# Layer 0's attention with the Hyena tiles in three parts per unit pair, and the filter's taps, norm and spectrum issued behind the first K tile

## The chip, the cores and the metric

The program runs on one core of one Trainium2 chip. The metric is the device time in microseconds (us) of one execution. TensorE (PE; PEld is its weight load), VectorE (DVE), ScalarE (ACT), GpSimd (POOL) and SyncE (SP) run programs of their own, written by hand, and meet only in semaphores.

## The reference, cut to what matters

Two blocks over 256 tokens of width 1024: two layers of a three-branch block (layer 0 also carries 256 context tokens, so 512 columns), then a second block. What the change touches is the beginning of layer 0:

```python
sh, sc, gt = modulation(c, ada_w[l], ada_b[l])          # silu(cond) @ ada_w: tiles "ada"
h  = rms_norm(x, norm_pre[l]) * (1.0 + sc[:, None]) + sh[:, None]
z  = h @ w_in[l]                                        # tiles k, q, v, hy, gu, gv, gate
y_a = diff_head_out(diff_attend(q, k_all, v_all, lam), da_subln[l], lam_init)
# hyena_filter: three small layers with sin between them, times a decay: the taps
hid = sin(freq[0] * (z0 @ w1 + b1)); hid = sin(freq[1] * (hid @ w2 + b2))
h   = (hid @ w3).reshape(L, 2, HY_WIDTH) * exp(-t * deltas)
# long_conv_bidir: k = taps / norm of the taps; irfft(rfft(u) * rfft(k))
```

The attention is differential: a unit is one head and 128 queries, with two score maps of 512 keys (tokens, units 0 to 7) or 256 keys (context, units 8 to 15); the weights are softmax(first) - lambda * softmax(second). Two units of one head make a pair, whose product with V is formed once.

## The kernel before

**Tiles.** All weights come as one stream of tiles of 128 x 1024 f32 (512 KB) through a ring of four `raw` buffers, which SP refills in order: tile t is fetched once tile t-4 has been used. For the large products ACT copies a tile to `whi` (fp32r, `act_hi`) and DVE forms `wlo` = raw - whi (`dve_lo`); PE then multiplies three times for each 128 rows, wlo by hhi, whi by hlo, whi by hhi (lines 372 to 374; 24 matmuls a tile with 512 columns), into one of four banks `gemm_bank`. "ada" tiles are used raw (line 430, two matmuls of 32 rows, four records). `pe_tiles(n)`, `act_tiles(n)`, `dve_tiles(n)` do the next n tiles of the stream on their engine: PE the products, ACT and DVE the evictions, and (unless `split=False`) each also prepares one tile further on. So the order of each engine's work is an order of calls written by hand.

**The front** (`pe_front`, `act_front`, `dve_front`) is all that comes before `h`. The modulation takes 16 ada tiles; after every four of them ACT copies the rows from PSUM (line 979), PE turns them (`pe_turn`, line 502) and DVE stores them (line 1487); after the fourth such group `dve_mod` makes `mod` and `modA` (lines 1705, 1706). Beside it run the RMS norm of x and ctx (ACT squares, line 947; PE sums, line 521; square root; DVE reciprocal, line 1370, and eight products, line 1552) and the filter: `hidden` twice (PE line 537, ten DVE instructions that reduce the argument of the sine, lines 1507 to 1501, ACT Sin line 1072), `taps` (PE line 547, four matmuls, then DVE products), their squares and norm (PE line 561), sum and difference, and `spec` (PE line 579, eight matmuls of 512 columns with K = 128), copied to `kre` and `kim` by `act_kern`. An f32 matmul of these shows as two records. Then `act_h`/`dve_h` build hhi and hlo from the eight slices k, alternating between ACT and DVE, and PE follows slice by slice in the first K tile (wait on `("h", 0)`), and goes on without waits through K, Q, V with the rotary step between them. POOL fetches `const_b` (the filter's constants and others) at once, and when it has landed the filter's third weight, the decay, the DFT matrices and the positions.

**Attention of layer 0** (`pe_attention`, `act_attention`, `dve_attention`). For unit u, DVE turns the exponentials into weights (line 1602), PE transposes them (line 656), ACT copies them (`wt`, line 1127), and after two units PE forms the product with V (line 666). Scores of unit u+1 (PE line 632) are taken to maxima by DVE (lines 1585 to 1587) and to exponentials by ACT (line 1115). Between these, each pair of units uses three tiles of the stream: one Hyena tile (`hy`, evicted by ACT line 1002 and DVE lines 1396, 1397) and two ada tiles of later groups. `pe_half` issues the Hyena tile's 24 matmuls in two halves, one in each unit:

```python
self.pe_half(u % 2)                 # 12 matmuls
...scores(u + 1); wait weights(u); transposes(u)
self.pe_tiles(2 * (u % 2))          # odd unit: two ada tiles, then the product with V
```

Of the kernel before, what the change touches and what calls it, by code (L numbers as in the profile page):

```python
# [17 lines left out]
TOK = 256  # L18
# [9 lines left out]
AHEAD_HI = 3  # L28
FILL = [1] * 8, [0, 1, 0, 1, 0, 1, 1, 1]
# [174 lines left out]
class Kernel:  # L204
# [177 lines left out]
    def pe_half(self, second):  # L382

        T, s = self.tiles[self.pe_next], self.tiles[self.pe_next].t % SPLIT
        if not second:
            self.pe.wait_ge(*self.at("tile_lo", T.t))
            self.pe_bank(T.use)
        for k in range(4 * second, 4 * second + 4):
            c = slice(k * P, (k + 1) * P)
            m = self.three(self.G[T.use % 4][:, 0:T.n], self.whi[:, s, c], self.wlo[:, s, c], self.hhi[:, k, 0:T.n], self.hlo[:, k, 0:T.n], k == 0, k == KT - 1)  # L390
        if second:
            m.then_inc(*self.mark("tile_used", "used", T.t))
            self.pe_next += 1
# [136 lines left out]

    def pe_hidden(self, l, s):

        pe, c = self.pe, self.c
        hid = self.tmp[0:64, 3, 0:TOK]
# [4 lines left out]
    def pe_taps(self, l):  # L539
        pe, hid = self.pe, self.tmp[0:64, 3, 0:TOK]  # L540
# [41 lines left out]
    def pe_front(self):  # L582
# [3 lines left out]
        pe.wait_ge(*self.landed("const_b"))  # L586
        self.pe_hidden(0, 0)
# [47 lines left out]
    def pe_attention(self, l):  # L635
# [5 lines left out]
        for u in range(n):  # L641
# [16 lines left out]
            self.pe_tiles(FILL[1][u] if l else 2 * (u % 2))  # L658
# [89 lines left out]
    def pe_block1(self, l):  # L748
        n = TOK if l else ALL
        self.pe_tiles(9)  # L750
# [319 lines left out]
    def act_hidden(self, l, s):  # L1070
        self.act.wait_ge(*self.at("hid_arg", l, s))
        self.act.activation(self.tmp[0:64, 3, 0:TOK], self.tmp[0:64, 3, TOK:ALL], ACT.Sin).then_inc(*self.mark("act_filter", "hid", l, s))
# [17 lines left out]
    def act_front(self):  # L1090
        act = self.act
        act.wait_ge(*self.at("cond_silu"))
        act.wait_ge(*self.landed("const_b"))
        self.act_hidden(0, 0)
        act.wait_ge(*self.landed("x"))
        act.wait_ge(*self.landed("ctx"))
        for k in range(KT):
            if k == 5:
                self.act_tiles(4, split=False)
            if k == 7:  # L1100
                self.act_hidden(0, 1)
            self.act_sq("x0", k, ALL, self.x[:, k, :]).then_inc(*self.mark("act_sq", "sq", "x0", k))
        self.act_root("x0", ALL)
        self.act_tap_sq(0)
        self.act_tiles(8, split=False)
        self.act_tap_root(0)
        self.act_tiles(4, split=False)
        for _ in range(AHEAD + 16):
            self.act_hi()

# [6 lines left out]
    def act_attention(self, l):  # L1117
# [4 lines left out]
        for u in range(n):  # L1122
            (q_off, k_off, nkeys), h, i = units[u]
            nkt = nkeys // P
            self.act_tiles(FILL[0][u] if l else u % 2)
# [1108 lines left out]
```

## Time and profile before

| | |
|---|---|
| median of 3 runs | 1651.92 us (1647.87 to 1652.4) |
| the profiled execution's own time | 1647.76 us |
| its span in the trace | 1646.5 us |
| PE busy | 1526.2 us (93%) |
| DVE, ACT busy | 892.5, 673.5 us |

The span is the traced part of the profiled execution, 1.26 us shorter than its time. Busy PE does not mean PE at full speed: TensorE's clock has two levels, and a stretch's "PEclk" is the mean granted level, 1.00 for 2.4 GHz and 0.50 for 1.2 GHz. Ends of matmuls are modelled, so that neighbouring rows can overlap by some 0.1 to 0.2 us; starts are recorded.

### The profile page before, as it was taken

The page shows a single profiled execution, that of the slowest core. Times are in us where ns is not written, and L with a number is a line of the kernel's source. Part 1 is how long each engine was busy: PE and PEld are TensorE (multiplying, and loading weights), DVE is VectorE, ACT ScalarE, POOL GpSimd, SP SyncE. Part 2 cuts the span into 40 slices and gives each one's busy share as a digit, 9 for nine tenths or more (in the row PEclk, how much of TensorE's full clock was granted, in tenths as well). Part 3 has the DMA queues.
Part 4 walks back from the last instruction along what each step waited for, and adds up shares of the span by engine and source line. Part 5 has one row for each costly group of instructions (what it writes and reads, how often), then busy time and mean ns, then how long its engine had stood idle before and what let it go on. Part 6 is the DMA issues. An engine that isn't in the chain of part 4 may idle for free.

```text
span 1646.5 us, 22242 instructions
## 1 busy us (share of the span) xinstructions
PE 1526.2 (93%) x9066; PEld 1274.4 (77%) x9066; DVE 892.5 (54%) x1573; ACT 673.5 (41%) x1175; POOL 32.5 (2%) x42
## 2 busy tenths in 40 slices
PE   5899989978999999969989999979989998999998
PEld 1587657756888887727778899968777778999997
DVE  3625563654532435466675675666543346666547
ACT  3423443133322223443454454556443444544434
POOL 0000000000000000100000000010000000100000
PEclk9899999998999999979999999999988999999999
DMA  7522332133323233133232455536421113555552
GB/s 289 173 75 74 130 127 91 52 110 124 106 90 102 90 103 97 53 125 116 86 107 90 160 187 184 178 94 205 128 93 61 52 52 128 180 183 188 188 185 78
DMA packets 57846, 203.14 MB, mean 123 GB/s; under 512 B 6256, under 2 KB 9456, under 8 KB 57616
## 3 DMA queue, kind: packets, MB, share of 16 engines
q1 hardware_dynamic: 55568, 194.01, 35.6%
q0 software_dynamic: 1888, 7.12, 1.2%
q8 instruction: 72, 1.18, 0.3%
q10 hardware_dynamic: 288, 0.58, 0.1%
q14 instruction: 30, 0.25, 0.0%
HBM read 200.65 MB, written 1.05 MB: 123 GB/s over the span
## 4 chain that ended last, share of the span: by engine, by line
PE 81%; DVE 11%; ACT 4%; DMA 2%; issue 1%; SPq 0%; ACTq 0%; DVEq 0%
PE gemm_bank L372 16%; PE gemm_bank L374 16%; PE gemm_bank L373 16%; PE misc_bank L372 6%; PE misc_bank L374 6%; PE misc_bank L373 6%; DVE wlo L1378 2%; PE misc_bank L818 2%; PE misc_bank L831 1%; PE misc_bank L521 1%; PE misc_bank L724 1%; PE misc_bank L717 1%; DMA raw<-in_stream 1%; DMA x<-in_ctx 1%; PE gemm_bank L430 1%
## 5 line engine op out<-in xcount | busy, mean ns | idle before, releaser
L372 PE MATMUL gemm_bank<-hhi,wlo 128*128 128x256 f32 (+1 forms) x1392 | 459.9, 330 | 45.0 <-DVE wlo L1378 21.5
L373 PE MATMUL gemm_bank<-hlo,whi 128*128 128x256 f32 (+1 forms) x1392 | 445.2, 320 | 0.0
L374 PE MATMUL gemm_bank<-hhi,whi 128*128 128x256 f32 (+1 forms) x1392 | 444.7, 319 | 0.0
L1378 DVE TENSOR_TENSOR wlo<-raw,whi 128x1024 fp32r<-128x1024 f32 x316 | 381.2, 1219 | 88.4 <-ACT whi L960 84.5
L960 ACT ACTIVATE whi<-raw 128x1024 fp32r<-128x1024 f32 x316 | 332.1, 1052 | 186.5 <-PE gemm_bank L374 122.9
L372 PEld LDWEIGHTS gemm_bank<-hhi,wlo 128*128 128x128 f32 x1392 | 274.7, 197 | 78.2 <-DVE wlo L1378 25.7
L373 PEld LDWEIGHTS gemm_bank<-hlo,whi 128*128 128x128 f32 x1392 | 274.8, 197 | 15.8 <-issue 0.7
L374 PEld LDWEIGHTS gemm_bank<-hhi,whi 128*128 128x128 f32 x1392 | 273.9, 197 | 16.8
L372 PE MATMUL misc_bank<-hhi,wlo 128*128 128x256 f32 (+1 forms) x496 | 160.7, 324 | 0.0
L373 PE MATMUL misc_bank<-hlo,whi 128*128 128x256 f32 (+1 forms) x496 | 160.7, 324 | 0.0
L374 PE MATMUL misc_bank<-hhi,whi 128*128 128x256 f32 (+1 forms) x496 | 160.7, 324 | 0.0
L372 PEld LDWEIGHTS misc_bank<-hhi,wlo 128*128 128x128 f32 x496 | 94.4, 190 | 7.5
L373 PEld LDWEIGHTS misc_bank<-hlo,whi 128*128 128x128 f32 x496 | 94.4, 190 | 7.5
L374 PEld LDWEIGHTS misc_bank<-hhi,whi 128*128 128x128 f32 x496 | 94.4, 190 | 7.4
L372 PE MATMUL gemm_bank<-arena_r,wlo 128*128 128x256 f32 (+1 forms) x280 | 89.5, 320 | 0.6 <-issue 0.6
L374 PE MATMUL gemm_bank<-arena_r,whi 128*128 128x256 f32 (+1 forms) x280 | 89.4, 319 | 0.0
L373 PE MATMUL gemm_bank<-arena_r,whi 128*128 128x256 f32 (+1 forms) x280 | 89.4, 319 | 0.0
L1413 DVE SCALAR_TENSOR_TENSOR tmp<-tmp,gemm_bank 128x512 f32<-128x512 f32 (+1 forms) x32 | 17.8, 555 | 109.7 <-ACT tmp L1021 109.7
L1021 ACT ACTIVATE tmp<-misc_bank 128x512 f32<-128x512 f32 (+1 forms) x40 | 20.5, 512 | 124.9 <-PE misc_bank L374 124.9
L372 PE MATMUL gemm_bank<-whi,hlo 128*128 128x512 f32 (+1 forms) x144 | 57.5, 399 | 1.3 <-ACT arena L984 1.3
L372 PEld LDWEIGHTS gemm_bank<-arena_r,wlo 128*128 128x128 f32 x280 | 53.3, 190 | 4.6 <-issue 0.8
L373 PEld LDWEIGHTS gemm_bank<-arena_r,whi 128*128 128x128 f32 x280 | 53.3, 191 | 3.8
(328 smaller groups left out, 1980.1 us busy)
## 6 DMA issues: line engine op xcount, KB each, us to landing
raw<-in_stream SPq DMA_DIRECT2D x364, 512.0 KB, 3.5
const_b<-in_const_b POOLq DMA_DIRECT2D x1, 1100.0 KB, 9.0
x<-in_x SPq DMA_DIRECT2D x1, 1024.0 KB, 11.4
x<-in_ctx SPq DMA_DIRECT2D x1, 1024.0 KB, 16.5
y<-in_hy_decay POOLq DMA_DIRECT2D x2, 512.0 KB, 7.3
arena<-in_gm_ws POOLq DMA_DIRECT2D x2, 512.0 KB, 5.6
y<-in_hy_w POOLq DMA_DIRECT2D x2, 256.0 KB, 4.9
shared<-in_dft POOLq DMA_DIRECT2D x1, 512.0 KB, 10.6
```

Of the source, the lines that this page charges most:

```text
L372: mm(out, w_lo, r_hi, start=first, stop=False)
L373: mm(out, w_hi, r_lo, start=False, stop=False)
L374: return mm(out, w_hi, r_hi, start=False, stop=last)
L430: m = pe.matmul(self.G[T.use % 4][c:c + 32, :], self.cond_w[:, 2 * q + kk, :], self.raw[:, T.t % RAW, kk * BR:(kk + 1) * BR], start=(q < 2 ...
L521: self.pe.matmul(self.sum_bank.get(stage, self.M[0])[:, 0:n], self.c["mean_all"], self.tmp[:, k % 2, 0:n], start=first, stop=last).then_in ...
L717: m = pe.matmul(b[:, :], self.dft[:, t, part * TOK + ft * P:part * TOK + (ft + 1) * P], ut[:, 2 * s + t, :], start=(t == 0), stop=(t == 1))
L724: m = pe.matmul(b[:, 0:TOK], spec[:, k, c * P:(c + 1) * P], self.idft[:, k, :], start=(k == 0), stop=(k == 3))
L818: mm(bank[:, c:c + nk], self.Z[r, qt, q_], self.Z[r, kt, 0:nk], start=True, stop=False)
L960: act.activation(self.whi[:, t % SPLIT, :], self.raw[:, t % RAW, :], ACT.Copy).then_inc(*self.mark("tile_hi", "tile_hi", t))
L1021: act.activation(self.tmp[:, e % 2, 0:n], self.M[e][:, 0:n], ACT.Tanh, scale=0.5).then_inc(*self.mark("act_sel", "sel_tanh", T.use))
L1378: dve.tensor_tensor(self.wlo[:, t % SPLIT, :], self.raw[:, t % RAW, :], self.whi[:, t % SPLIT, :].bitcast(F32), ALU.subtract).then_inc(*se ...
L1413: self.own(dve.scalar_tensor_tensor(th, th, 1.0, b[:, 0:n], ALU.add, ALU.mult))
```

## The change

Three things are moved; no arithmetic changes, but for where the hidden values of layer 0's filter lie (`y` in place of `tmp`).

In the attention, a pair's Hyena tile is issued in three parts of 2, 4 and 2 slices k (6, 12 and 6 matmuls); the two ada tiles stand before the odd unit's transposes, the third part between these and the product with V. ACT prepares the next Hyena tile's `whi` before the even unit's `wt`, DVE its `wlo` right after the odd unit's maxima, and DVE evicts the finished Hyena tile in the next pair's even unit.

In the front, the two hidden layers come later and with ada tiles and sums of squares around them; taps, norm and spectrum leave it. They stand in the new `pe_first`, `act_first`, `dve_first`, between the tiles of K and Q.

POOL fetches `const_b` only when x has landed, the filter's weight and decay only after the second group's store, the DFT matrices and positions only after `mod`.

```diff
+PARTS = (0, 2, 6, 8)
+    def pe_part(self, T, part):          # in place of pe_half
+        s = T.t % SPLIT
+        if part == 0:
+            self.pe.wait_ge(*self.at("tile_lo", T.t))
+            self.pe_bank(T.use)
+        for k in range(PARTS[part], PARTS[part + 1]):
...
 def pe_front(self):
         self.pe_tiles(2)
-        pe.wait_ge(*self.landed("const_b"))
-        self.pe_hidden(0, 0)
         pe.wait_ge(*self.landed("const_a"))
         for k in range(3):
             self.pe_sum("x0", k, ALL)
-        self.pe_hidden(0, 1)
         self.pe_tiles(2)
+        for k in range(3, 5):
+            self.pe_sum("x0", k, ALL)
         self.pe_turn(0, 0)
-        for k in range(3, KT):
+        self.pe_sum("x0", 5, ALL)
+        self.pe_tiles(2)
+        for k in range(6, KT):
             self.pe_sum("x0", k, ALL)
-        self.pe_tiles(2)
-        self.pe_taps(0)
+        pe.wait_ge(*self.landed("const_b"))
+        self.pe_hidden(0, 0)
         self.pe_tiles(2)
         self.pe_turn(0, 1)
         self.pe_tiles(4)
         self.pe_turn(0, 2)
-        self.pe_tiles(3)
+        self.pe_hidden(0, 1)
+        self.pe_tiles(4)
+        self.pe_turn(0, 3)
+
+    def pe_first(self):
+        self.pe_tiles(1)
+        self.pe_taps(0)
+        self.pe_tiles(4)
         self.pe_tap_norm(0)
+        self.pe_tiles(2)
+        self.pe_spec(0)
         self.pe_tiles(1)
-        self.pe_turn(0, 3)
-        self.pe_spec(0)
...
 def pe_attention(self, l):                # l == 0
-                self.pe_half(u % 2)
-            if l == 0 and u in (4, 8, 12):
-                self.pe_turn(*self.LATE_ADA[u // 4 - 1])
+                T = self.tiles[self.pe_next]
+                self.pe_part(T, u % 2)
             if u + 1 < n:
                 self.pe_scores(l, u + 1)
+            if l == 0 and u % 2:
+                self.pe_next += 1
+                self.pe_tiles(2)
             pe.wait_ge(*self.at("weights", l, u))
...transposes
-            self.pe_tiles(FILL[1][u] if l else 2 * (u % 2))
+            elif u % 2:
+                self.pe_part(T, 2)
+            elif u in (4, 8, 12):
+                self.pe_turn(*self.LATE_ADA[u // 4 - 1])
...
 def act_first(self):
+        self.act_tiles(3)
+        self.act_tap_sq(0)
+        self.act_tiles(2)
+        self.act_tap_root(0)
+        self.act_tiles(2)
+        for i in range(4):
+            self.act_kern(0, i)
+        self.act_tiles(1)
...
 def dve_front(self):
+        self.dve_turned(0, 0)
         v.wait_ge(*self.landed("const_b"))
         self.dve_hidden(0, 0)
-        self.dve_hidden(0, 1)
-        self.dve_turned(0, 0)
-        self.dve_taps(0)
-        self.dve_tap_sd(0)
-        self.dve_tap_add(0)
         self.dve_rstd("x0", ALL)
         self.dve_turned(0, 1)
...eight products
+        self.dve_turned(0, 2)
+        self.dve_hidden(0, 1)
         self.dve_tiles(16, split=False)
         self.dve_turned(0, 3)
         self.dve_mod(0)
...
 def gpsimd_program(self):
+        pool.wait_ge(*self.landed("x"))
         pool.dma_start(self.const_b[:], ins["const_b"])...
+                pool.wait_ge(*self.at("evac", self.extra["ada", 0, 1]))
                 self.pool_filter(0)
+                pool.wait_ge(*self.at("mod", 0))
                 pool.dma_start(self.dft, ins["dft"])...
```

Three places in the engines' own order show it. On TensorE at the program's start (L430 an ada tile, L521 a sum of squares, L502 a turn, L537 or L540 a hidden layer, L547 the taps), before and after together:

```order
-L537 MATMUL misc_bank<-const_b 64x256
 L521 MATMUL misc_bank<-tmp,const_a 128x512 x3
-L537 MATMUL misc_bank<-tmp,const_b 64x256
 L430 MATMUL gemm_bank<-raw,cond_w 32x512 x4
+L521 MATMUL misc_bank<-tmp,const_a 128x512 x2
 L502 MATMUL gemm_bank<-const_a 128x2 x4
-L521 MATMUL misc_bank<-tmp,const_a 128x512 x5
+L521 MATMUL misc_bank<-tmp,const_a 128x512
 L430 MATMUL gemm_bank<-raw,cond_w 32x512 x4
-L547 MATMUL misc_bank<-y,tmp 128x512 x4
+L521 MATMUL misc_bank<-tmp,const_a 128x512 x2
+L540 MATMUL misc_bank<-const_b 64x256
```

The taps' four matmuls leave this stretch, the hidden layers move down, and ada tiles and sums stand ahead of them.

On VectorE in the attention, before, from the second maximum taken in an odd unit to the next unit's weights (512 keys; L1597 to L1602 weights, L1585 to L1587 maxima, L1396 and L1397 the Hyena tile's eviction, L1378 the next tile's wlo):

```order
L1586 TENSOR_REDUCE stat<-misc_bank 128x1
L1587 TENSOR_SCALAR stat<-stat 128x2
L1396 SCALAR_TENSOR_TENSOR arena<-gemm_bank,const_b,arena 128x2x255
L1397 SCALAR_TENSOR_TENSOR arena<-gemm_bank,const_b,arena 128x2x255
L1378 TENSOR_TENSOR wlo<-raw,whi 128x1024
L1597 RECIPROCAL stat<-stat 128x2
L1598 TENSOR_TENSOR stat<-stat,lam_e 128x1
L1599 TENSOR_SCALAR tmp<-tmp,stat 128x512
L1602 SCALAR_TENSOR_TENSOR tmp<-tmp,stat 128x512
```

The same place in the changed kernel, up to the end of the even unit (L1636 to L1641 weights, L1624 to L1626 maxima, L1411 wlo, L1429 and L1430 the eviction):

```order
L1625 TENSOR_REDUCE stat<-misc_bank 128x1
L1626 TENSOR_SCALAR stat<-stat 128x2
L1411 TENSOR_TENSOR wlo<-raw,whi 128x1024
L1636 RECIPROCAL stat<-stat 128x2
L1637 TENSOR_TENSOR stat<-stat,lam_e 128x1
L1638 TENSOR_SCALAR tmp<-tmp,stat 128x512
L1641 SCALAR_TENSOR_TENSOR tmp<-tmp,stat 128x512
L1624 TENSOR_REDUCE stat<-misc_bank 128x1
L1625 TENSOR_REDUCE stat<-misc_bank 128x1
L1626 TENSOR_SCALAR stat<-stat 128x2
L1429 SCALAR_TENSOR_TENSOR arena<-gemm_bank,const_b,arena 128x2x255
L1430 SCALAR_TENSOR_TENSOR arena<-gemm_bank,const_b,arena 128x2x255
```

The wlo now follows the maxima at once, and the eviction has gone behind the even unit's maxima.

On ScalarE in the attention, one pair of units of 256 keys, before and then after (L1127 or L1158 wt, L1115 or L1143 the exponentials, L960 or L981 whi, L1002 or L1023 the Hyena tile's eviction, L1133 or L1168 the product's copy):

```order
L1127 ACTIVATE y<-misc_bank 128x2x128
L1115 ACTIVATE tmp,stat<-misc_bank,stat 128x256 x2
L960 ACTIVATE whi<-raw 128x1024
L1002 ACTIVATE arena<-gemm_bank,const_b 128x512
L1127 ACTIVATE y<-misc_bank 128x2x128
L1115 ACTIVATE tmp,stat<-misc_bank,stat 128x256 x2
L1133 ACTIVATE y<-misc_bank 128x256
```

```order
L981 ACTIVATE whi<-raw 128x1024
L1158 ACTIVATE y<-misc_bank 128x2x128
L1143 ACTIVATE tmp,stat<-misc_bank,stat 128x256 x2
L1158 ACTIVATE y<-misc_bank 128x2x128
L1143 ACTIVATE tmp,stat<-misc_bank,stat 128x256 x2
L1023 ACTIVATE arena<-gemm_bank,const_b 128x512
L1168 ACTIVATE y<-misc_bank 128x256
```

The whi has moved ahead of the even unit's wt, and the eviction behind the exponentials.

## Rows read from the trace of the kernel before

**Rows 1.** The page: the chain that ended last, by engine.

```profile
PE 81%; DVE 11%; ACT 4%; DMA 2%; issue 1%; SPq 0%; ACTq 0%; DVEq 0%
```

**Rows 2.** Windows: length, busy PE, PEld, DVE, ACT, POOL; PEclk, DMA share, GB/s.

```profile
0.00:24.50 24.50, 9.65 (x22) 2.50 (x23) 6.10 (x23) 6.71 (x11) 3.54 (x10) 1.00 0.95 344
24.50:58.30 33.80, 26.58 (x117) 10.67 (x117) 19.48 (x35) 10.77 (x18) 0.00 (x0) 0.85 0.63 227
58.30:71.70 13.40, 11.61 (x36) 6.26 (x34) 10.29 (x20) 10.59 (x20) 0.00 (x0) 1.00 0.29 94
71.70:108.00 36.30, 36.25 (x160) 30.03 (x161) 10.73 (x9) 12.88 (x18) 0.00 (x0) 1.00 0.35 116
138.00:246.30 108.30, 101.02 (x488) 66.11 (x488) 62.24 (x146) 49.92 (x113) 0.00 (x0) 1.00 0.31 108
721.50:742.00 20.50, 10.02 (x26) 6.08 (x26) 16.58 (x35) 8.85 (x19) 0.00 (x0) 0.56 0.20 74
```

**Rows 3.** DMA issues of the first 60 us: count, size, median us to landing.

```profile
raw<-in_stream SPq DMA_DIRECT2D x21, 512.0 KB, 4.4
...
x<-in_ctx SPq DMA_DIRECT2D x1, 1024.0 KB, 16.5
```

**Rows 4.** Timeline of the front: start, length, instruction, idle before.

```profile
12.53 0.54 DVE L1507 TENSOR_SCALAR tmp<-misc_bank,const_b 64x256 f32<-64x256 f32 x1 [1.93 <-PE misc_bank L537]
...
16.25 1.28 ACT L1072 ACT_TABLE_LOAD   x1 [6.11 <-DVE tmp L1501]
...
18.96 1.15 ACT L947 ACTIVATE tmp<-x 128x512 f32<-128x512 f32 x2 [1.00 <-DMA x<-in_ctx]
...
27.20 4.79 PE L521 MATMUL misc_bank<-tmp,const_a 128*128 128x512 f32 x10
...
43.11 3.35 DVE L1370 RECIPROCAL tmp<-tmp 128x512 f32<-128x512 f32 x1
...
46.57 2.49 DVE L1552 TENSOR_TENSOR arena<-x,tmp 128x512 f32<-128x512 f32 x4
...
55.97 0.60 ACT L979 ACTIVATE const_a<-gemm_bank 128x512 f32<-128x512 f32 x1 [0.73 <-PE gemm_bank L430]
...
58.19 0.17 DVE L1706 SCALAR_TENSOR_TENSOR modA<-mod,const_a 128x16 f32<-128x16 f32 x1
```

**Rows 5.** TensorE groups from 32 to 66 us, shapes apart.

```profile
L579 PE MATMUL misc_bank<-arena,shared 128*128 128x512 f32 x16 | 7.1, 597 | 0.0
...
L547 PE MATMUL misc_bank<-y,tmp 64*128 64x512 f32 x8 | 3.7, 602 | 0.0
...
L561 PE MATMUL misc_bank<-const_a,arena 128*128 128x1 f32 x8 | 1.1, 253 | 0.0
```

**Rows 6.** Waits of the attention, 125 to 270 us: total, times, longest.

```profile
PE gemm_bank L372 <- DVE wlo L1378: 5.8, 7, 1.2
...
PE misc_bank L656 <- DVE tmp L1602: 1.3, 4, 0.7
```

**Rows 7.** Timeline of the first units and of a later pair.

```profile
151.30 0.75 DVE L1396 SCALAR_TENSOR_TENSOR arena<-gemm_bank,const_b,arena 128x510 f32<-128x510 f32 x1 [3.81 <-ACT arena L1002]
...
154.34 0.66 PE L656 MATMUL misc_bank<-const_a,tmp 128*128 128x128 f32 x4
...
158.84 0.69 DVE L1585 TENSOR_REDUCE stat<-misc_bank 128x1 f32<-128x512 f32 x1
...
159.47 1.07 PE L430 MATMUL gemm_bank<-raw,cond_w 128*32 128x512 f32 x8
...
160.46 1.99 PE L666 MATMUL misc_bank<-y,arena 128*128 128x256 f32 x8
...
161.68 1.21 DVE L1378 TENSOR_TENSOR wlo<-raw,whi 128x1024 fp32r<-128x1024 f32 x1
...
213.13 0.50 PE L372 MATMUL gemm_bank<-hhi,wlo 128*128 128x512 f32 x1 [1.20 <-DVE wlo L1378]
```

**Rows 8.** Tiles of the ring in the attention, 205 to 250 us.

```profile
DMA to landing us min/median/max: 3.5/4.4/5.4
```

More of the change, by code:

```diff
@@ L380, in pe_bank @@
         return self.G[use % 4]
-    def pe_half(self, second):
-        T, s = self.tiles[self.pe_next], self.tiles[self.pe_next].t % SPLIT
-        if not second:
+    def pe_part(self, T, part):
+        s = T.t % SPLIT
+        if part == 0:
             self.pe.wait_ge(*self.at("tile_lo", T.t))
             self.pe_bank(T.use)
-        for k in range(4 * second, 4 * second + 4):
+        for k in range(PARTS[part], PARTS[part + 1]):
             c = slice(k * P, (k + 1) * P)
             m = self.three(self.G[T.use % 4][:, 0:T.n], self.whi[:, s, c], self.wlo[:, s, c], self.hhi[:, k, 0:T.n], self.hlo[:, k, 0:T.n], k == 0, k == KT - 1)
-        if second:
+        if part == 2:
             m.then_inc(*self.mark("tile_used", "used", T.t))
-            self.pe_next += 1
     def pe_feature(self, T, bank, hi, lo, begun=None, col=0):
@@ L539, in pe_taps @@
     def pe_taps(self, l):
-        pe, hid = self.pe, self.tmp[0:64, 3, 0:TOK]
+        pe, hid = self.pe, self.hid(l)
         pe.wait_ge(*self.at("hid", l, 1))
@@ L749, in pe_block1 @@
         n = TOK if l else ALL
-        self.pe_tiles(9)
+        if l == 0:
+            self.pe_first()
+        self.pe_tiles(9 if l else 1)
         for a, b in ROPE:
@@ L1071, in act_hidden @@
         self.act.wait_ge(*self.at("hid_arg", l, s))
-        self.act.activation(self.tmp[0:64, 3, 0:TOK], self.tmp[0:64, 3, TOK:ALL], ACT.Sin).then_inc(*self.mark("act_filter", "hid", l, s))
+        self.act.activation(self.hid(l), self.tmp[0:64, 3, TOK:ALL], ACT.Sin).then_inc(*self.mark("act_filter", "hid", l, s))
     def act_tap_sq(self, l):
@@ L1091, in act_front @@
         act = self.act
-        act.wait_ge(*self.at("cond_silu"))
-        act.wait_ge(*self.landed("const_b"))
-        self.act_hidden(0, 0)
         act.wait_ge(*self.landed("x"))
@@ L1099, in act_front @@
                 self.act_tiles(4, split=False)
-            if k == 7:
-                self.act_hidden(0, 1)
             self.act_sq("x0", k, ALL, self.x[:, k, :]).then_inc(*self.mark("act_sq", "sq", "x0", k))
         self.act_root("x0", ALL)
-        self.act_tap_sq(0)
-        self.act_tiles(8, split=False)
-        self.act_tap_root(0)
+        self.act_tiles(4, split=False)
+        self.act_hidden(0, 0)
+        self.act_tiles(4, split=False)
+        self.act_hidden(0, 1)
         self.act_tiles(4, split=False)
@@ L1124, in act_attention @@
             nkt = nkeys // P
-            self.act_tiles(FILL[0][u] if l else u % 2)
+            if l:
+                self.act_tiles(FILL[0][u])
+            elif u % 2 == 0:
+                self.act_hi()
             act.wait_ge(*self.at("w_turned", l, u))
@@ L1129, in act_attention @@
                 self.act_exps(l, u + 1)
-            self.act_tiles(FILL[1][u] if l else 2 * (u % 2))
+            if l:
+                self.act_tiles(FILL[1][u])
+            elif u % 2:
+                self.act_tiles(1, split=False)
+                self.act_tiles(2)
             if i == 1:
@@ L1201, in act_block1 @@
         self.act_h(l)
-        if l == 0:
-            for i in range(4):
-                self.act_kern(0, i)
         if l:
@@ L1213, in act_block1 @@
         else:
-            self.act_tiles(12)
+            self.act_first()
+            self.act_tiles(4)
         if l == 0:
@@ L1560, in dve_front, with dve_first @@
             self.dve_lo()
+    def dve_first(self):
+        self.dve_tiles(2)
+        self.dve_taps(0)
+        self.dve_tiles(1)
+        self.dve_tap_sd(0)
+        self.dve_tiles(1)
+        self.dve_tap_add(0)
+        self.dve_tiles(1)
+        self.dve_tap_rs(0)
     def dve_trig(self):
@@ L1606, in dve_attention @@
                 self.dve_maxima(l, u + 1)
-            self.dve_tiles(FILL[1][u] if l else 3 * (u % 2))
+            if l:
+                self.dve_tiles(FILL[1][u])
+            elif u % 2:
+                self.dve_lo()
+                self.dve_lo()
+            elif u:
+                self.dve_tiles(2, split=False)
+                self.dve_tiles(1)
             if l == 0 and u in (4, 8, 12):
@@ L1612, in dve_attention @@
         if l == 0:
-            self.dve_tiles(1)
+            self.dve_tiles(2, split=False)
+            self.dve_tiles(2)
             self.dve_turned(*self.LATE_ADA[3])
@@ L1768, in dve_block1 @@
         else:
-            self.dve_tiles(9)
+            self.dve_first()
+            self.dve_tiles(4)
         for a, b in ROPE:
```

10 lines of the change are left out of this document (6 added, 4 removed).

## The prediction

> **What bounds the kernel now.** I read the chain that ended last first. TensorE holds 81% of it [rows 1], so what counts is how long TensorE waits, and how much work is put where it does not wait. Then the windows over layer 0's beginning [rows 2]. From 71.7 us on TensorE is saturated (36.25 us busy of 36.3, 160 matmuls, so 0.227 us each). Before that it is not what sets the time: from 24.5 to 58.3 us it is busy 26.6 of 33.8 us with short work, and from 58.3 to 71.7 us the slices of h set the pace. In the attention (138 to 246.3 us) it is busy 101.0 of 108.3 us, 7.3 us idle. The waits of that stretch say on what: 5.8 us on DVE's wlo in 7 waits, 1.3 us on DVE's weights [rows 6]. The timeline shows the first kind: the wlo of 1.21 us starts at 161.68 us, when TensorE is already in the product with V (160.46, 1.99 us), because DVE evicts the finished Hyena tile first; a later pair then starts at 213.13 us after 1.20 us of idling [rows 7].
>
> **The front: when does h start?** Before, `modA` ends at 58.19 + 0.17 = 58.4 us [rows 4]. I walk the new order.
>
> First the data. ctx landed 16.5 us after its issue, just before the first square at 18.96 us [rows 3, 4]. Up to 24.5 us the DMA engines moved 344 GB/s in the mean [rows 2]. Ahead of ctx remain x, two tiles of the stream, and the two small constants, with ctx some 3.7 MB; const_b (1100 KB, 1.13 MB) starts only with x landed, and perhaps 0.4 MB of it still gets between: 4.1 MB / 344 GB/s = 12.0 us. If only const_b's own bytes are saved, ctx lands at 18.9 - 3.3 = 15.6 us. I take 13.0, nearer the first, because the filter's DMAs, issued behind const_b, are gone from this stretch too.
>
> The Trainium skill bears on this (DMA: Bandwidth & Descriptors, section Queues, rings and completion order): each DMA engine takes turns between the queues that have work. By that rule const_b on GpSimd's queue halves the share of x and ctx as long as it lasts, and the filter's DMAs do so after it. The long landing of ctx beside a stream tile's 4.4 us agrees, and it speaks for the earlier of the two values.
>
> From the first square to the last sum TensorE and ScalarE took 27.20 + 4.79 - 18.96 = 13.0 us [rows 4]. The new order has nearly the same things in it (one hidden layer less, two ada tiles more), so the last sum ends near 26.1 us, and the first hidden layer's matmul 0.6 us later: 26.7.
>
> From there DVE sets the pace: the sine's argument 3.6 us (12.53 to 16.15, [rows 4]), the reciprocal 3.35 us and 0.1, a store 0.2, eight products 2 x 2.49 = 5.0, a store 0.2, the second argument 3.6: 42.8 us. Then the Sin 0.5 and, behind it in ScalarE's order, the copy of the last rows; from that copy's start to `modA`'s end it took 58.4 - 55.97 = 2.4 us [rows 4]. Sum: 45.7 us, against 58.4: h is 12.7 us earlier. The rest of the stretch, 13.4 us from there until TensorE runs without waits at 71.7 [rows 2], has the same instructions.
>
> The ada tiles must have come through by then. Bytes before the last are 14.1 MB less 2.0 MB; by the order above TensorE frees the last four buffers near 30 to 32 us (my estimate: after the sums, the first hidden layer and a turn), a tile lands 4.4 us later [rows 3], so they are used up near 37 us, against 43 when ScalarE needs them. The cover is some 5 us; if it went, each further us would be a us of the front. Bounds: 9.5 us gained (ctx at 15.6) to 14.5 (sums without waits).
>
> **What comes back.** Taps, norm and spectrum were 3.7 + 1.1 + 7.1 = 11.9 us of TensorE [rows 5], placed where it had time (the spectrum during the first slices of h). Ends overlap the next row by 0.1 to 0.2 us each, so 11.5 us. Now they stand between K and Q tiles, in the saturated stretch, and are paid in full. Their DVE and ACT parts (taps, sums, squares, kern copies) lie under tiles of 24 x 0.227 = 5.4 us, in a stretch where DVE is busy 10.7 and ACT 12.9 of 36.3 us [rows 2], and their data land 25 us ahead: nothing.
>
> The clock: before, the spectrum filled the time before the first K tile, and the clock is at 1.00 from 58.3 to 71.7. Now TensorE is mostly idle from 37 to 48 us. Layer 1's start shows what that does: from 721.5 to 742 us, busy 10.0 of 20.5, the clock averages 0.56 (mostly the 1.2 GHz level), then it is back [rows 2]. The first K tile's slices arrive slower than either level needs; only what remains at low clock after the last slice costs: 0 to 3.4 us (half of 6.8); I take 0.5.
>
> The Trainium skill (TensorE: Matmul & The Clock Gate, section HAM oscillation) says the same against this change: idle gaps send the array back to half rate, and the next burst starts cold. Its price stays inside these bounds, as the burst is fed by h.
>
> Front in sum: -12.7 + 11.5 + 0.5 = **-0.7 us** (bounds: -14.5 + 11.5 = -3.0, and -9.5 + 11.9 + 3.4 = +5.8).
>
> **The attention.** *Waits on wlo (5.8 us):* the next tile's wlo now follows the odd unit's maxima. Counting from the scores' end in the odd unit, with durations of [rows 7]: maxima 1.5 (two of 0.69 and a small one), wlo 1.2, done after about 3 us; TensorE meanwhile has two ada tiles 1.1, transposes 0.7, the third part 6 x 0.227 = 1.4, and the product 2.0 (half with 256 keys): 4.2 to 5.2 us. So they go. *Waits on weights (1.3 us):* in odd units the ada tiles cover them; they go, but for the first unit. There DVE cannot begin the weights before it has evicted the Hyena tile of before (151.30 us), and the transposes start at 154.34 us as soon as they are done [rows 7]. Until then TensorE now has 6 matmuls less: 6 x 0.227 + the 0.1 idle of before = 1.5 us of new wait. *More switches:* one more break in the tile's matmuls per pair; the first matmul after a break takes 0.50 us by [rows 7] with its fill, and costs near 0.1 us at its neighbour's start: 8 x 0.1 = 0.8. *Whi ahead of wt:* ScalarE now waits for the raw tile before it copies the weights and forms the exponentials. Its tile is freed by the ada tiles of the pair before, 5.5 (256 keys) to 7 us ahead of the need; landing takes 3.5 to 5.4 us [rows 8] and whi 1.05. That is just hidden, and by the same counting the exponentials have 0.3 to 0.9 us of slack before the next scores. Nothing taken; at worst 0.5 us in each of 8 pairs.
>
> Attention in sum: -7.1 (the two waits) + 1.5 + 0.8 = **-4.8 us** (bounds: without the first wait -6.3, with 0.5 us more in each pair -0.8).
>
> **Sum.** -0.7 - 4.8 = -5.5 us on the profiled execution's 1647.76 (span 1646.5 and 1.26 around it): 1642.3 us. The median of the runs is 1651.92, 0.25% above this execution; the same 0.33% off it gives 1646.4 us.
>
> **The rivals.**
> *Slower: the whi ahead of the wt.* ScalarE's program is in order, so a raw tile that lands late stops wt, exponentials and with them the scores. The price is what exceeds the slack of about 1 us, in seven pairs. To bring the sum 5 us above before it must eat 5.5 + 5 = 10.5 us, 1.5 us a pair: tiles landing after about 8 us. The longest was 5.4 us [rows 8], and one wait of ACT on a tile already exists in that stretch. At 8 us: 1657 us.
> *The front loses.* It is the stream of ada tiles, not DVE, that ends it, and h gains only the bytes taken out of it. 2.0 MB at the 227 GB/s of 24.5 to 58.3 us [rows 2] give 8.7 us instead of 12.7, and the low clock may add 1 to 3. The front costs 3 to 5 us and the attention gives them back: 1650 us, no measurable change.
> *More than forecast.* DVE's chain starts earlier, as sums run without waits and h gains 14.5 us, and the first unit's wait is all that is left: 1647.76 - 3.0 - 5.5 gives 1639.3, by the median's ratio 1643.4 us.
> *The change does nothing in the attention*, since TensorE merely waits elsewhere in the pair (exponentials behind the copy of wt): front -0.7 alone, 1651 us.
>
> **How the numbers follow.** Forecast case (front about even, gaps closed, 3.5 to 8 us gained): 0.50. More than forecast: 0.13. Front loses: 0.16. Nothing in the attention: 0.09. Slower rival, with other mishaps of that size: 0.12. A no-change measurement can tell about 0.3%, 5 us. The forecast case straddles that line (5.5 expected): 0.36 of its 0.50 above it. Of the second all 0.13, and of the front rival 0.02. Faster 0.51; slower 0.13 (the slower rival, and 0.01 of the front's); same 0.36. Range: 1639 to 1655. Below lie gains over 13 us, above them half of the slower rival.
>
> **What would show it.** h's first slices near 48 us; TensorE without waits from near 59 us; taps, norm and spectrum between K and Q tiles without idling; in the attention no waits on wlo, one of 1.5 us on the first weights. Wrong would be: `modA` later than 49 us, waits of ScalarE for raw tiles, TensorE at 0.50 beyond 62 us, or new waits on exponentials.

## The result

The changed kernel takes 1639.43 us in the median of 4 runs (1637.06 to 1640.57), the kernel before beside it 1649.95 us (1647.87 to 1652.4): ratio 0.9927, 95% interval 0.9904 to 0.9949. It is faster by 10.5 us by the medians and by 12 us by the ratio; the forecast was 5.5 us (1646.4 us against 1651.92), and the value lies just inside the range. Measured again beside the last experiments it takes 1637.97 us against 1652.45, ratio 0.9913 (0.9896 to 0.9931). The ratios here and below have intervals of their own; they can differ by 0.1% from the quotient of the two medians, and a difference of that size means nothing.

The profiled execution has a span of 1635.7 us against 1646.5. First the line of its page on the chain that ended last, by engine: DVE's share has fallen from 11% to 8% [rows 1].

```profile
PE 84%; DVE 8%; ACT 4%; DMA 2%; issue 1%; SPq 0%; ACTq 0%
```

The windows of the same execution, with the columns of [rows 2]. They are cut where the changed kernel has its stages: shortly behind `modA` (46.6), behind the first K tile with its last slice of h (60.6), the saturated tiles after it, and the attention.

```profile
0.00:24.50 24.50, 12.97 (x40) 4.47 (x44) 2.92 (x15) 7.22 (x13) 0.88 (x5) 1.00 0.89 326
24.50:46.60 22.10, 15.53 (x80) 5.32 (x72) 15.88 (x33) 7.47 (x11) 1.28 (x3) 0.92 0.90 311
46.60:60.60 14.00, 8.54 (x25) 5.18 (x25) 10.88 (x19) 11.47 (x19) 1.37 (x3) 0.76 0.50 177
60.60:107.60 47.00, 47.00 (x190) 34.78 (x190) 16.56 (x19) 16.83 (x24) 0.00 (x0) 1.00 0.27 90
137.60:236.60 99.00, 97.53 (x489) 66.06 (x489) 61.26 (x143) 48.22 (x112) 0.00 (x0) 1.00 0.34 119
```

From 60.6 us on TensorE has no idle time (47.00 of 47.00 us); before, that began at 71.7. In the attention 7.3 us of idling have become 1.5. The front in the timeline: ctx is there for the first square at 13.47 us (18.96 in [rows 4]), the last ada tile comes at 41.63, `modA` at 45.92 (58.19), and DVE's chain between ctx and `modA` runs in the forecast's order.

```profile
13.47 1.15 ACT L968 ACTIVATE tmp<-x 128x512 f32<-128x512 f32 x2 [4.11 <-DMA x<-in_ctx]
...
41.63 1.05 PE L430 MATMUL gemm_bank<-raw,cond_w 128*32 128x512 f32 x4 [1.14 <-DMA raw<-in_stream]
...
45.92 0.17 DVE L1753 SCALAR_TENSOR_TENSOR modA<-mod,const_a 128x16 f32<-128x16 f32 x1
```

And the attention: the new first wait (153.95), and a pair, where the product with V runs into the next tile's matmuls without a gap. [rows 7] has the same product of the kernel before (160.46) with its wlo still to come, and at 213.13 a wait behind a product of 256 keys.

```profile
153.95 0.66 PE L670 MATMUL misc_bank<-const_a,tmp 128*128 128x128 f32 x4 [1.47 <-DVE tmp L1641]
...
159.89 1.22 DVE L1411 TENSOR_TENSOR wlo<-raw,whi 128x1024 fp32r<-128x1024 f32 x1
...
161.24 1.89 PE L685 MATMUL misc_bank<-y,arena 128*128 128x256 f32 x8
...
162.78 0.58 PE L373 MATMUL gemm_bank<-hhi,wlo 128*128 128x512 f32 x1
```

The last two rows' times matter: the next tile's first matmul starts 1.54 us after the product does, though the row gives the product 1.89 us. Ends of matmuls are modelled, and this one reaches 0.35 us over the next start, more than the 0.1 to 0.2 us that I had counted on. The same two places before, for 512 and for 256 keys:

```profile
162.95 0.50 PE L372 MATMUL gemm_bank<-hhi,wlo 128*128 128x512 f32 x1 [0.49 <-DVE wlo L1378]
...
210.80 1.13 PE L666 MATMUL misc_bank<-y,arena 128*128 128x256 f32 x4
```

From start to start they took 2.49 us (from 160.46) and 2.33 us (to 213.13).

### The profile page after: what moved, and what is told of

Its sections match the earlier page's. It is cut to its first block, busy times and chain, and to the rows that moved or that the text cites. A ratio compares the mean times of both kernels' runs of the same rounds, so it can differ in the third digit from the quotient of the medians.

```text
span 1635.7 us, 22244 instructions
## 1 busy us (share of the span) xinstructions
PE 1521.8 (93%) x9066; PEld 1274.2 (78%) x9066; DVE 892.1 (55%) x1573; ACT 675.0 (41%) x1176; POOL 32.5 (2%) x42
## 3 DMA queue, kind: packets, MB, share of 16 engines
HBM read 200.65 MB, written 1.05 MB: 123 GB/s over the span
## 4 chain that ended last, share of the span: by engine, by line
PE 84%; DVE 8%; ACT 4%; DMA 2%; issue 1%; SPq 0%; ACTq 0%
PE gemm_bank L373 17%; PE gemm_bank L375 16%; PE gemm_bank L374 16%; PE misc_bank L373 6%; PE misc_bank L375 6%; PE misc_bank L374 6%; PE misc_bank L839 2%; PE misc_bank L521 1%; DMA raw<-in_stream 1%; PE misc_bank L852 1%; DVE wlo L1411 1%; PE misc_bank L743 1%; PE misc_bank L736 1%; PE gemm_bank L430 1%; PE misc_bank L685 1%
## 5 line engine op out<-in xcount | busy, mean ns | idle before, releaser
L1411 DVE TENSOR_TENSOR wlo<-raw,whi 128x1024 fp32r<-128x1024 f32 x316 | 380.7, 1218 | 77.4 <-ACT whi L981 73.3
L981 ACT ACTIVATE whi<-raw 128x1024 fp32r<-128x1024 f32 x316 | 332.2, 1052 | 193.8 <-PE gemm_bank L375 123.0
```

The costliest lines, as they stand in the source:

```text
L981: act.activation(self.whi[:, t % SPLIT, :], self.raw[:, t % RAW, :], ACT.Copy).then_inc(*self.mark("tile_hi", "tile_hi", t))
L1411: dve.tensor_tensor(self.wlo[:, t % SPLIT, :], self.raw[:, t % RAW, :], self.whi[:, t % SPLIT, :].bitcast(F32), ALU.subtract).then_inc(*se ...
```

## Where the time went

The attention is measured from the first scores' start to the start of the head norm's sums; "V to next" is the sum, over the 8 pairs, of the distance from the start of the product with V to the start of the next tile's first matmul. All values are starts, read from each trace's timeline.

| execution | modA | first scores | attention | V to next | rest of it |
|---|---|---|---|---|---|
| before | 58.19 | 143.64 | 109.19 | 18.15 | 91.04 |
| changed | 45.92 | 143.25 | 99.87 | 8.86 | 91.01 |

So of 10.8 us of span 0.4 came from the front, 9.3 from the attention, and all of these 9.3 in one place: V to next fell from 2.49, 2.38, 2.39, 1.85, 2.33, 2.33, 2.33 and 2.05 us to 1.54 four times and 0.67 to 0.68 four times. The idling that the trace shows at these places before is only 5.8 us, in seven of the eight [rows 6]. The other 3.5 us, 0.45 in each of the seven and 0.31 in the eighth, stood in no idle row: 0.35 (0.21 in the eighth) is the overlap above, which a wait takes away, and 0.10 is the product itself, 1.99 us behind two ada tiles [rows 7] and 1.89 behind the third part.

The rest of the stage took the same time in sum, but not in its pieces. From the start of each kind of work to the start of the next (a wait counts to the work ahead of it):

| execution | Hyena matmuls | scores | transposes | ada tiles | turns |
|---|---|---|---|---|---|
| before | 58.04 | 15.27 | 6.25 | 7.97 | 3.51 |
| changed | 59.57 | 15.08 | 5.10 | 7.97 | 3.31 |

The added breaks cost 1.5 us. The scores hold the first unit's new wait, +1.5 us from start to start, and have lost the waits on weights, -1.7. The transposes gain 1.15 us: with ada tiles behind them they took 0.59 us (512 keys), with Hyena matmuls behind them 0.41.

The last 1.1 us of the span lie behind the attention; there, from the head sums to the span's end, the executions of all kernels here took between 1389.3 and 1400.6 us, and both executions of the kernel before (1393.6 and 1390.4) differ by more than this, so it stands for nothing.

## The experiments

**One half of the change at a time.** First the attention with its parts in the kernel before, its front untouched:

```diff
+PARTS = (0, 2, 6, 8)
...
-                self.pe_half(u % 2)
+                T = self.tiles[self.pe_next]
+                self.pe_part(T, u % 2)
...
```

(and so on through the three attention functions, as the change has them; `pe_front`, `act_front`, `dve_front` and GpSimd's program stay as before).

> The kernel before with the new attention alone (three parts, ada tiles moved, DVE's and ACT's new order); the front is that of before. From the first scores to the head sums the kernel before takes 109.2 us and the changed one 99.9. Theory 1: the whole 9.3 us belong to the attention, and half of it is what TensorE's windows did not show as idle, since each wait on wlo also costs the emptying of the array behind the product with V. Then this stretch takes 99.9 us here too, and the kernel is 9 to 10 us faster (ratio near 0.994). Theory 2: the forecast's 4.8 us are right for the attention, and the rest comes from the front, whose transfers and DVE work no longer stand close before it. Then the stretch takes 104 us or more and the kernel gains about 5 us.

Measured: 1640.02 us against 1650.91, ratio 0.9948 (0.9926 to 0.997). The attention took 100.25 us, V to next 8.86. Then the other half, the changed kernel with the three attention functions and `pe_half` of before put back:

> The changed kernel with the attention of before (two halves, old order on DVE and ACT): the front and the moved taps, norm and spectrum alone. Theory 1: the front is nearly even, 12 us earlier and 11.7 us given back: the attention's first scores come 0.4 us earlier than before, the attention takes 109.2 us, and the time is that of before (-0.4 us, same). Theory 2: the front brings about 5 us, through later stretches.

Measured: 1648.68 us, ratio 0.998 (0.9955 to 1.0006); `modA` at 46.10, first scores at 144.13, the attention 109.33 us. The two ratios multiply to 0.9928, the change's own is 0.9927. With intervals of some 0.2% to each side that is closer than it had to come, but no interaction of the halves shows, and the attention holds most of the gain. Whether the front gains anything by itself this interval leaves open.

**The order on DVE alone.** The wlo of the next tile before the eviction of the finished one, in the kernel before and behind the new front:

```diff
-            self.dve_tiles(FILL[1][u] if l else 3 * (u % 2))
+            if l:
+                self.dve_tiles(FILL[1][u])
+            elif u % 2:
+                self.dve_lo()
+                self.dve_lo()
+                self.dve_tiles(2, split=False)
+                self.dve_tiles(1)
```

> The kernel before with one edit: in the odd units of layer 0 DVE makes the next Hyena tile's wlo before it evicts the finished one; halves and ada tiles stay. Theory 1 (the order of wlo is all that counts, and a wait on it costs more than its idle time): from the product with V to the next tile's first matmul TensorE takes 1.54 us (512 keys) and 0.68 us (256 keys) in place of 2.4 and 2.33; the stretch from the first scores to the head sums falls from 109.2 to about 99.5 to 100.5 us; 9 us faster. Rival: the three parts and the moved ada tiles are needed, since they cover the weights and the copy of them; then the gain is at most the 5.8 us of the waits on wlo.

> The changed kernel's front with the attention of before and the one edit of the run before this one (wlo ahead of the eviction). Theory 1: 9 to 10 us faster than before, level with the changed kernel, and without its wait of 1.5 us on the first weights, but with the waits on weights of before (1.3 us). The rival: 5 to 6 us faster.

Measured: 1640.93 us, ratio 0.995 (0.9931 to 0.9968), and with the new front 1638.28 us, ratio 0.993 (0.9901 to 0.9959). In both the attention took 101.49 us, 7.7 less than before, and V to next 10.02 (1.64 four times, 0.78 to 0.89 four times: the 0.10 behind ada tiles is still there). Four lines on DVE are worth 7.7 of the 9.3 us. That is more than the 5.8 us which the rival allowed and 1 to 2 us less than the first theory had.

**The three parts without the wlo's order.** The change, with DVE's old order put back:

```diff
-            elif u % 2:
-                self.dve_lo()
-                self.dve_lo()
-            elif u:
-                self.dve_tiles(2, split=False)
-                self.dve_tiles(1)
+            else:
+                self.dve_tiles(3 * (u % 2))
...
```

> The changed kernel, with one part undone: after an odd unit's maxima DVE again evicts the finished Hyena tile before it forms the next tile's wlo. The three parts, the ada tiles ahead of the transposes and ScalarE's order stay. It tells apart whose gain the 9.3 us of the attention is, and what a wait on TensorE costs beside the idling that the profile shows. Theory (a wait behind the product with V costs its shown idling and some 0.45 us more of the array's emptying): waits on wlo come back in most pairs; the product now starts 1.4 us later than before, behind the third part, while DVE's eviction must wait for that part's end, so that the wlo comes 1.3 (eviction with its start) + 1.2 us behind the third part, against a product of 1.9 us (1.1 with 256 keys): shown idling near 0.5 and 1.2 us, and from the product's start to the next tile 2.4 and 2.3 us where the change has 1.54 and 0.68. The attention from first scores to head sums takes 8 to 10 us more than with the change: 108 to 110 us, the execution 1646. Rival (the three parts by themselves give cover, and wlo's order is a detail): the distance stays within 0.3 us of 1.54 and 0.68, the attention at 100 to 102 us, 1638.

Measured: 1675.13 us in one run, against 1652.45 for the kernel before; the attention 129.11 us. Both theories missed the size, and the first has the place. The waits of this stretch (from 136 to 275 us, total, times, longest), and one of them in the timeline:

```profile
PE gemm_bank L373 <- DVE wlo L1411: 19.6, 8, 2.7
```

```profile
221.26 1.02 PE L685 MATMUL misc_bank<-y,arena 128*128 128x256 f32 x4
...
224.99 0.79 PE L373 MATMUL gemm_bank<-hhi,wlo 128*128 128x512 f32 x1 [2.70 <-DVE wlo L1411]
225.58 0.63 PE L374 MATMUL gemm_bank<-hlo,whi 128*128 128x512 f32 x1
```

V to next became 31.2 us (4.18 three times, 3.75, 3.73 four times), 22.3 above the change. Its eight waits show 19.6 us of idling, and 8 x 0.35 = 2.8 make up the rest: the overlap is lost once per wait (the row of 1.02 us and the 2.70 of idling fill the 3.73 us between the two starts, against 0.67 in the change). DVE's eviction waits for ScalarE's part of it (line 1023), to which ScalarE comes only behind the exponentials, so the wlo is later than I reckoned. The remaining 6.9 us are clock. They lie in the Hyena matmuls (5.3) and the scores (1.6) behind the waits, and no new wait stands in them. The matmul behind the wait has neighbours of 0.63 us where the change has 0.39, the granted clock from 136 to 275 us averages 0.94, and rows of that length stand behind five of the eight waits.

The new places on TensorE and ScalarE are thus a loss of some 20 us without the wlo's order and a gain of 1.6 us with it. Three things are in these figures together, the three parts, the ada tiles' place and ScalarE's whi ahead of the wt; no run tells the parts' own share.

**Where the ada tiles stand.** They go from ahead of the transposes to behind the third part:

```diff
-            if l == 0 and u % 2:
-                self.pe_next += 1
-                self.pe_tiles(2)
             pe.wait_ge(*self.at("weights", l, u))
...
             elif u % 2:
                 self.pe_part(T, 2)
+                self.pe_next += 1
+                self.pe_tiles(2)
```

> The changed kernel with the two ada tiles of each pair back behind the odd unit's transposes (after the third part, before the product with V). Theory 1 (only wlo's place counts): the waits on wlo stay away, and only the four to five waits of 0.15 to 0.67 us on the odd units' weights come back: 101.2 us from first scores to head sums instead of 99.9. Rival: the moved ada tiles also carried the cover of wlo, and waits on wlo return; 103 us or more.

Measured: 1648.65 us in one run. Neither theory held: the waits on wlo stayed away, as the first had it, but the loss in the attention was some nine times as large (11.8 us instead of 1.3). The attention took 111.71 us, V to next 9.96, the rest of it 101.75, so 10.7 us were lost outside the place that the change mended. Among the waits of the stage (150 to 256 us) are 25.3 us of ScalarE's for raw tiles; in the change these are 8.9 us, 2.0 the longest (125 to 260 us). The second row is TensorE's wait for the weights, of which 1.5 us are the first unit's.

```profile
ACT whi L980 <- DMA raw<-in_stream: 25.3, 8, 4.2
...
PE misc_bank L667 <- DVE tmp L1640: 5.9, 6, 2.1
```

One of these waits in the timeline, followed to TensorE: the raw tile arrives, ScalarE makes the whi, copies the weights (0.37 us) and forms two exponentials, and only then come the scores, after 1.14 us of idling.

```profile
217.21 1.06 ACT L980 ACTIVATE whi<-raw 128x1024 fp32r<-128x1024 f32 x1 [3.58 <-DMA raw<-in_stream]
218.17 0.37 ACT L1157 ACTIVATE y<-misc_bank 128x256 f32<-128x256 f32 x1
218.43 0.47 ACT L1142 ACTIVATE tmp<-misc_bank,stat 128x256 f32<-128x256 f32 x1
218.88 0.47 ACT L1142 ACTIVATE tmp<-misc_bank,stat 128x256 f32<-128x256 f32 x1
...
219.50 0.70 PE L644 MATMUL misc_bank<-arena 64*128 64x256 f32 x4 [1.14 <-ACT tmp L1142]
```

That is the chain of the slower rival, made real: the ada tiles release their buffers of the ring later, the next raw tile lands later, and ScalarE, with whi ahead of wt, stands. In the change the same wait exists (2.0 us) and stays inside the slack. Two other things are in the 10.7 us. The ada tiles no longer cover the weights, a share that was not measured apart. And some 3 us are clock: from 220.6 to 225 us the granted clock is 0.62 and the pair's ada tiles take 1.87 us from start to next start instead of 1.00, and the same again behind the wait at 244.40.

**The first wait.** The eviction of the Hyena tile that stands ahead of the first unit goes behind the first weights and the second maxima, and only the wlo stands ahead of them:

```diff
-        self.dve_tiles(1)
+        if l:
+            self.dve_tiles(1)
+        else:
+            self.dve_lo()
...
+            else:
+                self.dve_tiles(1, split=False)
```

> The changed kernel with one edit on DVE: the Hyena tile that stands ahead of the first unit is evicted behind the first weights and the second maxima instead of ahead of them. Theory 1: the wait of 1.47 us on the first unit's weights is all that the three parts cost; it goes, and from the first scores to the head sums the stretch falls from 99.9 to 98.4 us. Rival: the eviction, now later, holds up the next weights or a bank, and the wait turns up in the second unit; the stretch stays at 99.9.

> The same kernel as the one with the first weights ahead of hy1's eviction, on the chip of this group, so that it can be compared with the change and with the late hidden layer. If the 1.5 us of first wait is all that it saves, its median lies 1.0 to 2.0 us below the changed kernel's of this group; if the wait goes elsewhere, within 0.5 us of it.

Measured: 1635.99 us, ratio 0.9914 (0.9884 to 0.9943), and measured again beside the last experiments 1633.29 us, ratio 0.9896 (0.9876 to 0.9917), where the changed kernel had 1637.97. The wait of 1.47 us is gone in both (attention 98.32 twice, transposes at 152.81 right behind the scores at 151.75). The medians of these last two differ by 4.7 us, which is more than these 1.5 us explain, and more than the 1 to 2 us expected; but the runs behind them spread over 10.8 and 6.6 us.

**const_b at once.** GpSimd no longer waits for x:

```diff
-        pool.wait_ge(*self.landed("x"))
         pool.dma_start(self.const_b[:], ins["const_b"]).then_inc(*self.landing("const_b"))
```

> The changed kernel, but GpSimd fetches const_b at once, as before; the filter's weight, decay and DFT matrices stay late. Theory 1 (const_b shares the DMA engines with x and ctx): ctx lands about 3 us later than in the changed kernel (first square near 16.5 us instead of 13.5), modA ends near 49 us instead of 46.1, and the first scores come 3 us later, near 146.3. Rival: the ada tiles set the front's end, whatever ctx does: the last one is used at 42.7 us there, 1 us ahead of the need; then modA moves by 1 us or less.

Measured: 1640.37 us in one run; the first square at 16.26 us instead of 13.47, `modA` at 49.74 (45.92), first scores at 146.89 (143.25). The DMA issues of the first 50 us, with the median from issue to landing:

```profile
x<-in_x SPq DMA_DIRECT2D x1, 1024.0 KB, 11.5
x<-in_ctx SPq DMA_DIRECT2D x1, 1024.0 KB, 13.8
```

In the changed kernel they land after 8.7 and 11.0 us. So const_b beside them costs 2.8 us; of the 5.5 us by which ctx comes earlier in the change (16.5 in [rows 3]) the other 2.7 are left, by subtraction, to the filter's DMAs and the order. In the kernel before, with const_b beside it, x landed after 11.4 us, as here. The Trainium skill (DMA: Bandwidth & Descriptors, section Queues, rings and completion order) says that each DMA engine serves in turn the queues that have work. The trace agrees: x itself is late by 2.8 us although nothing was put ahead of it in its own queue.

**The second hidden layer late.** On top of the early first weights, DVE forms the layer's argument, and ScalarE its Sin, behind the first K tiles:

```diff
         self.dve_turned(0, 2)
-        self.dve_hidden(0, 1)
         self.dve_tiles(16, split=False)
...
         self.dve_tiles(2)
+        self.dve.wait_ge(*self.at("h", 0, KT - 1))
+        self.dve_hidden(0, 1)
+        self.dve_tiles(1)
         self.dve_taps(0)
...
-        self.pe_tiles(1)
+        self.pe_tiles(3)
         self.pe_taps(0)
```

(ScalarE's Sin likewise, and the tiles behind are shared out anew).

> The kernel with the first weights ahead of hy1's eviction, and besides it the second hidden layer's argument and Sin taken out of the front's chain: DVE forms the argument, and ScalarE the Sin, behind the first K tiles, with the taps' matmuls two tiles later. Theory A (DVE's chain ends the front): modA's end comes 3.6 us (the argument) earlier than 46.1, as long as the stream's last ada tile, used at 42.7, leaves room: mod can't be formed before 44.5 or so, so 1 to 1.5 us is gained, first scores near 142, the execution 1634.5 to 1635.5. Theory B (the stream of ada tiles is what ends the front, with DVE's argument in its shadow): nothing, first scores within 0.3 us of 143.3 to 143.7, and 1636. Rival on the other side: the argument's 3.6 us of DVE between the first K tiles make an eviction or a wlo late in the saturated stretch, 1 to 3 us lost, 1637 to 1639.

Measured: 1635.69 us, ratio 0.9895 (0.9878 to 0.9912), beside 1633.29 without it: no difference that can be measured. In its profile `modA` starts at 44.66, 2.3 us behind the last ada tile's matmuls (42.38), with only the copy of their rows and their turn between, so the stream ends the front once DVE's argument is out of the way. The first scores come at 142.78, the earliest here. Against the changed kernel's first execution that is 1.3 us at `modA`, as theory A has it, and 0.5 at the scores. One profile can't settle the size, since the new front's own executions spread over 1.4 us, and the whole kernel's time doesn't show it.

**Both kernels again.** For the scatter of the front:

> The kernel before once more, for one profile. Two kernels with the front of before had their first scores at 144.8 and 147.6 us, against 143.6 in its first profile, and in both the spectrum's matmuls ran partly at the low clock (16 records over 9.2 and 8.0 us instead of 6.6). Theory: this is the old front's spread, since its short bursts leave the clock's level to chance; here again between 143.6 and 148. The three profiles with the new front had 143.3, 144.0 and 144.1. Rival: the first profile is the rule, 143.6 within 0.5 us.

> The changed kernel once more, as the group's own measure: ratio to the kernel before 0.992 to 0.994 if the 10 to 12 us of the first measurement is the change's own; above 0.996 if that measurement was lucky. First scores between 143.2 and 144.1 if the new front starts the saturated stretch independently of the clock, up to 147 if it scatters as the front before does (143.6 to 147.9 in its executions).

Measured: before 1648.9 us in one run, first scores at 147.94; changed 1637.97, first scores at 144.24. The windows of the kernel before, first in this execution, with the columns of [rows 2]:

```profile
0.00:24.50 24.50, 9.18 (x17) 2.46 (x17) 6.10 (x23) 6.21 (x10) 3.57 (x10) 0.79 0.96 342
...
46.60:60.60 14.00, 10.66 (x42) 3.84 (x35) 5.68 (x12) 1.99 (x4) 0.00 (x0) 0.62 0.76 267
```

The four executions with the old front have first scores at 143.64, 144.83, 147.59 and 147.94 us, with `modA` at 58.19, 59.28, 62.13 and 62.51. The two late ones have a granted clock of 0.62 from 46.6 to 60.6 us, where the first had 0.88. Ahead of `modA` the execution above has the tap norm at 1.87 us instead of 1.05, the ada tile behind it at 1.92 instead of 1.05 and the last turn at 1.84 instead of 1.02. These are 2.5 of the 4.3 us by which its `modA` is late. The rest had come before, up to an ada tile at 53.85 (52.52 in the first execution) that had waited 1.46 us for its raw tile instead of 0.36. So the old front's end hangs on TensorE's short work and on the tiles behind it. The eight executions with the new front and const_b behind x have `modA` from 45.92 to 47.36 and first scores from 143.25 to 144.47, although their granted clock from 46.6 to 60.6 us is 0.63 to 0.76, for what TensorE does then waits for h. In the mean the new front begins the attention at 144.02 us, the old one at 146.00.

## Why the prediction was right and wrong

**Wrong: the attention's term.** The step that failed is the price of the waits, "Waits on wlo (5.8 us)" and "Waits on weights (1.3 us)", taken together as -7.1 us from the rows of idling. A wait was priced by its idling, but the idling counts from the modelled end of the matmul ahead, and where nothing is waited for the next matmul starts before that end (0.35 us behind the product with V). From start to start the waits on wlo were worth 8.5 us and those on weights 1.7, together -10.2. A second term was put at nothing: products, transposes and turns that no longer touch ada tiles are shorter by 0.8, 1.15 and 0.2 us, -2.1 in all. The new wait on the first weights was right (1.5 us), and the breaks cost 1.5 where 0.8 was taken. Sum: -10.2 - 2.1 + 1.5 + 1.5 = -9.3 us, where the prediction has -4.8 and its bounds end at -6.3.

**Right, with the sizes.** `modA`'s end 46.1 us (45.7 forecast), ctx at 13.5 (13.0), the first hidden layer 27.1 (26.7), the last sine and reciprocal chain as reckoned. What comes back was 11.7 us (11.5): the last slice of h is 12.1 us earlier and the first scores 0.4. The low clock after 46 us cost nothing that shows, since TensorE waited for slices of h behind it (1.42 us at 57.25). The front gave -0.4 us against -0.7 in the profiled pair. That closeness is partly luck: the profile before was the earliest of four executions of the old front, whose first scores spread over 4.3 us. In the mean of all executions the new front is 2.0 us earlier, for the reason above, which the prediction did not see. The medians of the front's half lie 2.2 us apart, but the interval of that ratio (0.9955 to 1.0006) does not exclude nothing.

**Nearly wrong.** The ada stream was used up at 42.7 us, not 37, and ScalarE came to the last rows at 43.71; the cover was 1 us and not 5. Tiles landed after 5.5 us in the median of the first 60 us, not 4.4 [rows 3], and TensorE waited for them at 32.3, 33.6 and 41.6 us.

**The rivals.** The slower one did not happen, but its mechanism is real: raw tiles made ScalarE wait 8.9 us in 7 waits without harm, and with the ada tiles some 2 us later in the pair these waits became 25.3 us and the rest of the stage lost 10.7 us. "The attention gives nothing" and "the front loses" are out by the two halves. "More than forecast" came nearest (1643.4 us), for a reason that wasn't the cause: it had h 14.5 us earlier, and h came 12.3 us earlier.

## What to carry to other kernels

Price a wait on the saturated engine from start to start, against the same pair of instructions where they run through. Idling read behind a modelled end misses the overlap, here 0.35 us per wait, nearly a third on top of a wait of 1.2 us. When a matmul group waits for a producer on an engine that works in order, look at what stands ahead of the producer there before splitting the group: here the order was worth 7.7 us, and the split with its other moves 1.6 us more; without the order they lost 20. A start-up that runs at either clock level should be judged over several executions.

## What the runs showed of the hardware

Short waits in a TensorE otherwise saturated were followed by the 1.2 GHz level. Without the wlo's order there are eight idle stretches of 1.86 to 2.71 us, one every 12 to 16 us, and behind five of them, all of 2.29 us or more, matmuls take 0.63 us where 0.39 is usual; behind two others of 2.29 and 2.71 us they do not. With the ada tiles behind the transposes the same rows stand from 221.65 us, behind idling of 1.14 and 0.47 us. Idling of 1.2 us in the kernel before left the clock at 1.00 [rows 2].

The same front, with the same instructions, was granted 1.00 over its first 24.5 us in two executions and 0.79 in two others. At that point the two of 0.79 were hardly later (the ada tile behind the second hidden layer at 24.73 and 25.02 us against 24.47 and 24.65), but they are the two whose `modA` came at 62.13 and 62.51 us instead of 58.19 and 59.28.
